# Hybrid decoder layer on one core: the merge and output gates computed as an exponential on ScalarE and two operations on VectorE, three gate buffers, and a third chunk loaded during the decode

## The reference

```
z = einsum('btd,de->bte', h, w_in)
mq, mk, mv, mo, mif, dq, dk, dv, gm, gd = split_columns(z)
...
# mLSTM branch: a scan over chunks, then
h = rms_norm(h, g_mlstm);  out = sigmoid(mo) * h
# merge of the two branches
merged = (sigmoid(gm) * einsum('btw,wd->btd', hm, w_proj_m)
          + sigmoid(gd) * einsum('btw,wd->btd', hd, w_proj_d))
y = einsum('btd,de->bte', merged, w_out)
```

## Time and profile before

| | |
|---|---|
| three timed executions | 1869.02, 1869.07, 1872.77 us |
| the profiled execution, its own time | 1871.06 us |
| the profiled execution, its span from first to last instruction | 1869.3 us |
| TensorE busy / VectorE / ScalarE / GpSimd | 1766.1 / 752.9 / 500.8 / 148.8 us |
| decode block | about 541.8 to 684.5 us |
| mLSTM block | about 684.5 to 848.1 us |
| mean granted TensorE clock | 0.984 |

### The profile page before, as it was taken

How to read it: one execution, slowest core, us unless ns; L and a number is a source line. 1 busy time by engine, 2 the same in 40 slices (tenths; PEclk the granted TensorE clock), 3 DMA queues, 4 the chain that set the end, 5 groups by cost and what they waited for, 6 DMA issues and landing times. The chain is left out here.

```text
span 1869.3 us, 27347 instructions
## 1 busy us (share of the span) xinstructions
PE 1766.1 (94%) x11470; PEld 1669.2 (89%) x11470; DVE 752.9 (40%) x1005; ACT 500.8 (27%) x805; POOL 148.8 (8%) x231
## 2 busy tenths in 40 slices
PE   6999899999979888888999999999999999999998
PEld 5899888888878778888987899999999999999997
DVE  5422144544420134434544544344244244244245
ACT  4311144434423224322133421211211211211212
POOL 4100000000010013310002220000000000000001
PEclk8999999999989999989999999999999999999999
DMA  9565333231228456406352121111111111111104
GB/s 335 196 198 181 106 121 101 93 113 60 84 75 256 123 178 175 134 28 150 134 177 90 51 83 50 41 47 47 45 47 46 46 47 46 46 46 46 46 26 165
DMA packets 159561, 190.40 MB, mean 102 GB/s; under 512 B 13677, under 2 KB 138109, under 8 KB 159420
## 3 DMA queue, kind: packets, MB, share of 16 engines
q1 hardware_dynamic: 135064, 168.85, 28.2%
q10 hardware_dynamic: 23368, 19.53, 3.3%
q0 software_dynamic: 1008, 0.23, 0.1%
HBM read 146.70 MB, written 41.87 MB: 101 GB/s over the span
## 5 line engine op out<-in xcount | busy, mean ns | idle before, releaser
L158 PE MATMUL ps<-mg_hi,w_hi 128*128 128x352 f32 x1008 | 218.5, 325 | 5.5 <-issue 2.5
L158 PE MATMUL ps<-mg_hi,w_lo 128*128 128x352 f32 x1008 | 217.3, 323 | 0.0
L158 PE MATMUL ps<-mg_lo,w_hi 128*128 128x352 f32 x1008 | 217.0, 323 | 0.0
L158 PEld LDWEIGHTS ps<-mg_hi,w_hi 128*128 128x128 f32 x1008 | 171.4, 189 | 7.2 <-issue 5.2
L158 PEld LDWEIGHTS ps<-mg_hi,w_lo 128*128 128x128 f32 x1008 | 173.0, 188 | 0.0
L158 PEld LDWEIGHTS ps<-mg_lo,w_hi 128*128 128x128 f32 x1008 | 171.2, 188 | 0.0
L143 DVE TENSOR_TENSOR w_lo<-w_raw,w_hi 128x2048 fp32r<-128x2048 f32 x61 | 141.3, 2316 | 52.4 <-ACT w_hi L139 52.4
L2694 DVE TENSOR_TENSOR f_t<-f_t,ps 128x1056 f32<-128x1056 f32 x80 | 100.3, 1253 | 151.2 <-PE ps L158 151.2
L139 ACT ACTIVATE w_hi<-w_raw 128x2048 fp32r<-128x2048 f32 x61 | 116.7, 1913 | 121.0 <-PE ps L158 120.0
L1283 PE MATMUL ps<-acts_hi,w_hi 128*128 128x352 f32 x384 | 132.3, 344 | 17.7 <-ACT gate_ev L1867 9.1
L1168 PE MATMUL ps<-acts_hi,w_hi 128*128 128x352 f32 x384 | 133.7, 348 | 9.1 <-PEq L327 4.8
(11 more groups left out here) (396 smaller groups left out, 3005.9 us busy)
## 6 DMA issues: line engine op xcount, KB each, us to landing
w_raw<-in_w_in SPq DMA_DIRECT2D x22, 1024.0 KB, 6.1
w_raw<-in_w_up SPq DMA_DIRECT2D x22, 1024.0 KB, 5.1
w_ada_chunks<-in_w_ada ACTq DMA_DIRECT2D x16, 1024.0 KB, 8.0
w_raw<-in_w_down SPq DMA_DIRECT2D x11, 1024.0 KB, 4.8
z_scratch<-out_z SPq DMA_DIRECT2D x48, 176.0 KB, 1.8
z_scratch<-gate_ev SPq DMA_DIRECT2D x48, 176.0 KB, 3.4
w_ada_chunks<-in_w_ada SPq DMA_DIRECT2D x8, 1024.0 KB, 10.0
z_scratch<-stage SPq DMA_DIRECT2D x12, 528.0 KB, 3.0
```

What stands on the lines that cost most here:

```text
L158: mm = pe.matmul(ps[:, bank + b, 0:TB], w[wi][:, k, j * P:(j + 1) * P], (a_hi, a_lo)[ai][:, k, b * TB:(b + 1) * TB], start=(n == 0), stop= ...
```

## The change

The logistic function is now 1 / (1 + exp(-x)): ScalarE computes exp(-x) in the same place where it computed the sigmoid, and VectorE adds 1 (with an upper bound, so that an infinity can't occur) and takes the reciprocal, both in place. That holds for the 48 gate tiles, for the four tiles of the prompt's output gate, and for the sample tokens' output gate. The gate buffers are three instead of two. Chunk 2 of the mLSTM operands is loaded in the decode block. Twelve of the 18 small loads of ScalarE's queue now stand behind the evacuation of gate tile 0, with a semaphore of their own (`d_norm`), and the four loads of `state_C` are issued by SyncE. To make room, `ct` and `kw` lie in the memory of `at`, and three tiles of the next block (`h_a`, `gate_m`, `gate_d`) are placed otherwise.

```diff
-    gate_stored = [sem("gate_stored0"), sem("gate_stored1")]
+    gate_evac, gate_rec = sem("gate_evac"), sem("gate_rec")
+    LOGIT_MAX = 3.0e38
+    GB = 3
+    gate_stored = [sem(f"gate_stored{i}") for i in range(GB)]
...
     def gate_out(sp, t, src):
-        sp.wait_ge(gate_evac, t + 1)
-        sp.dma_start(ZT[...], src).then_inc(gate_stored[t % 2], 16)
+        sp.wait_ge(gate_rec, 2 * (t + 1))
+        sp.dma_start(ZT[...], src).then_inc(gate_stored[t % GB], 16)
+
+    def gate_invert(dve, t):
+        ev = gate_ev[:, t % GB, :]
+        dve.wait_ge(gate_evac, t + 1)
+        dve.tensor_scalar(ev, ev, 1.0, LOGIT_MAX, ALU.add, ALU.min).then_inc(gate_rec, 1)
+        dve.wait_ge(gate_rec, 2 * t + 1)
+        dve.reciprocal(ev, ev).then_inc(gate_rec, 1)
...
@@ decode block, SyncE
+                pes.wait(sp, ("sc", DEC_B - 1))
+                for b in range(0, DEC_B, 2):
+                    sp.dma_start(C[:, b:b + 2, :, :], I["state_C"][0, b:b + 2]...).then_inc(d_c, 16)
...
-                for i, (dst, src) in enumerate(chunk_loads(0) + chunk_loads(1)):
-                    until(AT_O + i)
+                for c in range(LS):
+                    for i, (dst, src) in enumerate(chunk_loads(c)):
+                        until(AT_O + 2 * (5 * c + i) // LS)
@@ decode block, ScalarE
-                    if t > 2:
-                        act.wait_ge(gate_stored[(t - 1) % 2], 16 * ((t - 1) // 2))
-                    act.activation(gate_ev[:, (t - 1) % 2, :], ps[...], ACT.Sigmoid).then_inc(gate_evac, 1)
+                    if t > GB:
+                        act.wait_ge(gate_stored[(t - 1) % GB], 16 * ((t - 1) // GB))
+                    act.activation(gate_ev[:, (t - 1) % GB, :], ps[...], ACT.Exp, scale=-1.0).then_inc(gate_evac, 1)
+                until(2)
+                for h in range(H):      # the twelve small loads, before this in front of the first gate tile
@@ decode block, VectorE
                 def gates(t):
+                    gate_invert(dve, t - 1)
...
-                until(DEC_TILES)
+                until(DEC_TILES + 1)
@@ mLSTM block, SyncE
                 until(M_TILE0 + 1)
-                load(2)
@@ mLSTM block, ScalarE (chunk 0)
                 def out_gates(h):
-                    nac.done(act.activation(mo_g[:, h], mo_g[:, h], ACT.Sigmoid), ("mo", h))
-                    nac.wait(act, ("mo", h))
+                    nac.done(act.activation(mo_g[:, h], mo_g[:, h], ACT.Exp, scale=-1.0), ("mo", h))
+
+                def out_gains(h):
+                    ndv.wait(act, ("mor", h))
                     nac.done(act.activation(mo_g[:, h], mo_g[:, h], ACT.Copy, scale=gain_t[:, h:h + 1]), ("mog", h))
...
                         out_gates(2)
                         out_gates(3)
+                        out_gains(0)
+                        out_gains(1)
                     until(AT_NEXT[c] + 1)
+                    if c == 0:
+                        out_gains(2)
+                        out_gains(3)
@@ mLSTM block, VectorE
+                def out_inverse(h):
+                    nac.wait(dve, ("mo", h))
+                    ndv.done(dve.tensor_scalar(mo_g[:, h], mo_g[:, h], 1.0, LOGIT_MAX, ALU.add, ALU.min), ("mod", h))
+                    ndv.wait(dve, ("mod", h))
+                    ndv.done(dve.reciprocal(mo_g[:, h], mo_g[:, h]), ("mor", h))
...
+                until, inverted = counted(gates, DEC_TILES + 1), counted(invert, DEC_TILES + 1)
...
+                    inverted(AT_NUM[c])     # in front of st(c)
...
+                    inverted(AT_TR[c])      # behind w(c+1)
+                    if c == 0:
+                        out_inverse(0)
+                        out_inverse(1)
+                    else:
                         out_cols(c - 1)
...
+                    if c == 0:              # behind hn(0)
+                        out_inverse(2)
+                        out_inverse(3)
+                    inverted(AT_NEXT[c])
```

More of the change, by code:

```diff
@@ L1514, in _ @@
                 dvs.done(dve.scalar_tensor_tensor(out=w_s[:], in0=ps[:, 4, 0:TS], scalar=SCALE_M, in1=d_s[:], op0=ALU.mult, op1=ALU.mult), "w")
+                acs.wait(dve, "o_gate")
+                mo_s = zs[:, Z_MO:Z_MO + H, :]
+                dvs.done(dve.tensor_scalar(mo_s, mo_s, 1.0, LOGIT_MAX, ALU.add, ALU.min), "o_den")
+                dvs.wait(dve, "o_den")
+                dvs.done(dve.reciprocal(mo_s, mo_s), "o_rec")
                 until(AT_K[0])
@@ L1591, in _ @@
                 pes.wait(dve, "h_cols")
+                dvs.wait(dve, "o_rec")
                 for h in range(H):
@@ L1732, in build @@
     CH = range(NCH)
-    OPEN = [x for h in range(H) for x in (("mo", h), ("mog", h))]
+    OPEN = [("mo", 0), ("mo", 1), ("mo", 2), ("mo", 3), ("mog", 0), ("mog", 1), ("mog", 2), ("mog", 3)]
+    OPEN_REC = [[x for h in (i, i + 1) for x in (("mod", h), ("mor", h))] for i in (0, 2)]
     NPE_STEPS = ([("kT", 0), ("vT", 0), ("s", 0)]
@@ L1746, in build @@
                                              + ([("w", c + 1)] if c + 1 < NCH else [])
[L1747 removed]
+                                             + (OPEN_REC[0] if c == 0 else [])
+                                             + ([("cols", c - 1)] if c else []) + [("ssum", c), ("ms", c), ("hn", c)]
+                                             + (OPEN_REC[1] if c == 0 else []))]
                   + [("cols", NCH - 1)])
@@ L1990, in _ @@
                 until(GATE_TILES + 1)
+                inverted(GATE_TILES + 1)
             @block.tensor
@@ L2136, in build @@
         sb("merged_home", [P, 2 * KT * T])
-        h_a = nc.alloc_sbuf_tensor_at("h_a", [P, 2, KT, P], F32, offset=nc.sbuf_base)
-        gate = [sb("gate_m", [P, T]), sb("gate_d", [P, T])]
-        gain = sb("gain_mix", [P, 2, D_MODEL])
+        gate_m, gain, gate_d = sb("gate_m", [P, T]), sb("gain_mix", [P, 2, D_MODEL]), sb("gate_d", [P, T])
+        gate = [gate_m, gate_d]
+        h_a = [nc.alloc_sbuf_tensor_at(f"h_a{i}", [P, KT, P], F32, offset=M_AT + 8 * KT * T + i * 4 * (T + 2 * D_MODEL)) for i in range(2)]
         stats = sb("stats_mix", [P, NTT, 6])
@@ L2165, in _ @@
                     sp.dma_start(branch[:, H + h], BRANCH[h]).then_inc(n_br[h % 2], 16)
-                for i in range(2):
-                    sp.wait_ge(gate_stored[i], 8 * GATE_TILES)
+                for i in range(GB):
+                    sp.wait_ge(gate_stored[i], 16 * ((GATE_TILES - i + GB - 1) // GB))
                 gate_load(0)
```

73 lines of the change are left out of this document (35 added, 38 removed).

## The result

Four timed executions of the changed kernel took 1892.79 us in the median (1888.51 to 1894.98), four of the kernel before 1870.92 us. The ratio is 1.0108, 95% interval [1.0089, 1.0127]: by it some 20 us slower, where 28 were forecast (1897 us, range 1873 to 1921).

The account below looks back on a forecast made before the run. TensorE, busy 1766 of 1869.3 us, was taken as the bound. Terms of 0.9 (entry to mLSTM block), 23.0 and 2.5 (chunk 0, clock), 1.0 (later chunks) and 1.2 (block's end) sum to 28.6; forecast 1869 + 28 = 1897 us, range 1873 to 1921.

Parts of the forecast that it names:

- The price of the reciprocal: VectorE's wide reciprocals: 6.5 ns a column, so 2.44 us for a gate tile and 6.8 us for an output-gate tile.
- The ends of the range: Reciprocal's cost bounds: 0.6 ns a column, rival at 1849 us, chance 0.14; 8.8 ns, rival at 1921 us, chance 0.14.
- the 4.7 of the 1- and 4-column rows: Rival on VectorE's reciprocal: 4.7 ns a column, with a smaller chunk 0 loss; 1880 us, chance 0.18.
- Chunk 0's stall: mLSTM block, before gate tile 29: TensorE late by 23.0 us, plus 2.5 us of reduced clock.
- The chain named in the prediction: mLSTM chunk 0: tile 28's evacuation follows gains in ScalarE's queue, which wait for VectorE's output-gate inversions; ends at 746.5.
- Chunks 2 to 7 and the end: mLSTM block: VectorE binds three-tile chunks, -5.7; `cols` +1.9; hn of chunk 7 +4.8; sum +1.0; block's end +1.2 us.
- Table loads: ScalarE: 19 of 23 go, 1.28 us each, counting only where TensorE waits behind one.
- Decode block: Gains of 8.3 us against 6.7 at its end and 2.5 of clock; mLSTM block entered 0.9 us later.
- The end of the decode block: VectorE's inversions delay the last gate store: +6.7 us, plus 2.5 us of reduced clock at TensorE's restart.
- the wait for `e_s`: Decode block's softmax: TensorE's whole 3.4 us wait goes, with about 1.7 us of low clock behind it.
- The first evacuation's wait: Decode block, gate tiles 0 and 1: TensorE's 2.4 us wait falls to 0.6 us, 1.8 gained.
- The ordinary reciprocal: Rival on VectorE: inversions cost 0.7 us, output-gate tiles 1.5, kernel about 20 us faster; 1849 us, chance 0.14.

Follow-up runs that it names:

- experiment 6: Changed kernel with ScalarE's four output-gate gains moved behind the evacuation of gate tile 28; 1891.7 us, ratio 1.0127 to the kernel before.
- experiment 11: Changed kernel with the prompt's output gate inverted chunk by chunk and its gain moved from ScalarE to VectorE; 1889.5 us, ratio 1.0126 to the kernel before.
- experiments 1 and 2: Changed kernel with the logistic function by tanh: first with one VectorE operation per gate, 1845.5 us; second with no VectorE operation for the gates, 1843.4 us.
- experiment 5: Changed kernel with sigmoids everywhere again, keeping three gate buffers, early chunk 2 and moved DMAs; 1842.6 us, ratio 0.9881 to the kernel before.
- experiment 4: Changed kernel with only the gate tiles back to a sigmoid, output gates still by exponential and reciprocal; 1874.4 us, ratio 1.0034 to the kernel before.
- experiment 8: Sigmoid kernel with three buffers, early chunk 2 and moved DMAs, but `state_C` loads on ScalarE again; 1849.3 us, ratio 0.9907 to the kernel before.
- experiment 3: Changed kernel with only the prompt's output gate back to sigmoid and gain on ScalarE; 1870.1 us, ratio 1.0009 to the kernel before.
- experiment 7: Sigmoid kernel with three buffers, early chunk 2 and moved DMAs, but twelve small loads before gate tile 0 again; 1850.3 us, ratio 0.9909 to the kernel before.

## Why the prediction was right, step by step

*The price of the reciprocal,* 6.5 ns a column taken from the slope between 2 and 4 columns, measured 6.25: 2.35 us and 6.55 us against 2.44 and 6.8. The ends of the range (0.6 and 8.8) and the 4.7 of the 1- and 4-column rows are out. There was luck in this: the slope rests on 14 ns between two small shapes, 1 and 2 columns showed none, and it was carried on to 1024 columns. That it came out within 4% could not be known from these rows, and the chances (0.50 for this case) said so. The rule that the Trainium skill states ("VectorE: DVE Perf Modes", "First, the fixed hardware budget": an iterative divide with a repeat count of 8, where an addition needs one slice) gave the direction; taken as eight steps an element it was too dear.

*Chunk 0's stall.* Forecast 23.0 us and the late evacuation of tile 28 done at 746.5 behind the gains; it ran from 746.40 to 746.85, and TensorE waited 28.05 us. That the two times agree so closely is in part chance: the time before the decode block was 3.5 us longer and the decode block 3.4 shorter than forecast. The ledger is the fairer measure: +24.2 against 25.5 with the clock at the entry. The chain named in the prediction is the one in the trace. But it isn't the only one: experiment 6 cut ScalarE's link out and lost nothing of the stall, and 11 shows that behind both lies the sum of VectorE's work. That VectorE becomes the bound was priced in chunks 2 to 7 only, and the place of the four wide pairs was taken for the cause of chunk 0.

*Chunks 2 to 7 and the end.* Forecast 72 us for the four chunks with three tiles; they took 72.8 (`hn` from 770.61 to 843.44). The low clock behind the stall cost 1.5 us (4 us at 0.62) instead of 2.5. hn of chunk 7 costs 3.1 instead of 4.8 (6.4 against 3.4 of wait), `cols` of chunk 0 in front of vT of chunk 3 has 0.9 of wait, 0.4 more than before, instead of 1.9, and the block's end costs 1.1 as forecast (6.80 against 5.66 at L158). In the ledger +2.1 against 4.7.

*Table loads.* Worth nothing in the sum; experiments 1 and 2 against 5 show it for a kernel with three buffers. 23 became four. By the page of the Trainium skill that the prediction cites, "ScalarE: Activation LUTs" (section "What ACT_TABLE_LOAD costs"), a drain beside each load would have doubled what they cost ScalarE. The trace doesn't show it: in experiment 4 a load runs from 734.20 to 735.48 and the evacuation starts at 735.49.

*Decode block.* Here the size was off most: 3.4 of the 8 us between forecast and result (the restart to tile 29 has 1.3 of them, what follows 2.6, the rest 0.8). The mLSTM block was to start about 1 us later than before; counted from the start of the decode block it came 5.0 earlier, or 2.6 with the low clock behind the restart. The end of the decode block cost +5.2 (after against experiment 5) and 2.4 of clock behind it, where 6.7 and 2.5 were forecast. The gain was 10.2 (experiment 5) instead of 8.3. The term that was too small is the wait for `e_s` with its low clock: forecast with 3.4 of wait and 1.7 of clock, it measured 6.5 together (experiment 8: 3.25 of wait and 3.1 of clock behind it). In the kernel before, the clock behind the wait cost only 1.7, as forecast, but its trace has a second stretch of low clock that was left out:

```profile
655.00:660.00 5.00, 3.81 (x29) 3.17 (x30) 1.85 (x7) 3.50 (x6) 0.00 (x0) 0.80 0.23 57
660.00:665.00 5.00, 5.00 (x35) 3.81 (x35) 1.94 (x3) 0.47 (x1) 0.00 (x0) 0.86 0.42 120
```

5 x 0.20 + 5 x 0.14 = 1.7 us, which experiment 5 and the changed kernel don't have (1.00 there). Experiment 8, with the wait back, doesn't have it either, so that it hangs on this wait is not shown. The first evacuation's wait also goes entirely (2.4), where 0.6 was thought to stay. 8.3 + 1.7 + 0.6 = 10.6, measured 10.2; undone one by one, the two parts give 2.8 + 6.5 = 9.3. Together with the smaller cost of the end this makes -5.0 instead of -1.6.

*The rivals.* The ordinary reciprocal (1849 us) was the right account of the case with a cheap operation: experiments 1 and 2 have it, with 1845.5 and 1843.4. Its gain was a few microseconds too small, as in the decode block. The 17 us that the prediction took for TensorE's need in a three-tile chunk was right: 16.8 in experiment 5.

Not settled: how much of the two kinds of inversion overlaps. Alone they cost 1.28% (experiment 3 against 5) and 1.53% (4 against 5), together 2.27% (after against 5): by the ratios 10 us are counted twice (an estimate from their intervals: give or take 6), by the traces from the first gate tile to the products (25.5 + 27.9 against 48.5) 5 us, and 2 if the clock that experiment 5 was lucky with is taken out (3 us).

## What to carry to other kernels

Before an operation is moved to an engine that looks idle, add up that engine's work in the block where it lands, not over the whole span: VectorE was 40% busy on the page of before, and 66 of 166 us in this block, but the change brought 92 us more, and TensorE needs only 149. If a table switch is to go, look for a function that the loaded table has: tanh gives the logistic function for one cheap operation behind it or none (the Trainium skill lists exp and tanh in one set, "ScalarE: Activation LUTs", "Table sets: the hidden batching unit"; with tanh the kernel has four loads, as with exp). And before one link of a stall is moved, look whether a second chain ends at the same engine: in experiment 6 the whole stall came back by other ways.

## What the runs showed of the hardware

- A reciprocal on VectorE costs the same 6.25 ns a column from 128 to 1024 columns; the 128x512 one of experiment 11, in four pieces of 128, took 3353 ns, on the same line (954 + 384 x 6.25 = 3354).
- Operations of VectorE were stretched where GpSimd worked beside them: in chunk 0 of the changed kernel hn took 1.74 us and an addition of 128x1024 1.53, where GpSimd had three operations of 128x512 from 727.3 to 731.7; in the earlier trace rows hn took 0.69 with GpSimd idle, and the other additions took 0.63. The pattern holds over the block, in the kernel before as in the changed one: hn took 1.7 to 1.8 us wherever GpSimd worked beside it and 0.69 where it was idle, the last two chunks among them. The reciprocal was not stretched: 6.55 us beside GpSimd's 730.01 to 731.72 as without. That they belong together was seen in the traces, not tested.
- Reduced clock behind a wait varies between executions. Behind the wait of 2.49 us before tile 29 the granted clock was 0.57 over four microseconds in experiment 7, and 1.00 in experiment 5, whose code is the same there. The 3.25 us wait of experiment 8 was followed by 0.56 over seven microseconds, the 3.42 us wait for `e_s` of the kernel before by 0.59 over 3.6 and 0.94 over the next four. So in these traces a wait of 2.5 to 3.4 us cost between nothing and about its own length once more, and this part was not the same in each. Why was not found.

The granted clock behind the same wait, experiment 7 first:

```profile
710.00:714.00 4.00, 3.96 (x15) 3.96 (x16) 0.97 (x2) 0.63 (x1) 0.00 (x0) 0.57 0.77 137
```

and experiment 5:

```profile
708.00:712.00 4.00, 3.92 (x24) 3.92 (x25) 1.00 (x2) 0.66 (x2) 0.00 (x0) 1.00 0.67 124
```
